# The second block's 116 projection and gate tiles: high weights times both token halves in one 512-column matmul

## What is computed

```
h = rmsnorm(x, norm_w[l])
proj = h @ w_in[l]
a_q, a_f, a_i, a_z, b_x, b_z, c_z, c_xbc, c_dt, gate_logits = jnp.split(proj, split_idx, axis=-1)
...   # three mixers: o_a (HGRN2), o_b (RG-LRU), o_c (SSD)
branch_out = jnp.einsum('bsnc,ncd->bsnd', branches, w_out[l].reshape(N_BRANCH, BRANCH_WIDTH, D_MODEL))
gates = jax.nn.sigmoid(gate_logits.astype(jnp.float32).reshape(bsz, s, N_BRANCH, D_MODEL))
x = x + jnp.sum(gates * branch_out, axis=2).astype(x.dtype)
```

## Time and profile before

| | us |
|---|---|
| median of 3 runs | 4380.95 (4380.47 to 4385.95) |
| the profiled execution | 4382.56 |
| its span in the trace | 4380.8 |
| PE busy in the span | 4246.8 |
| stage with the 232 halves, first to last matmul | 3456.2 to 4218.5 |

### The profile page before, as it was taken

One profiled execution on the slowest core, in us unless ns is written; L12 is line 12 of the kernel. 1 busy time (PEld: TensorE's weight loads), 2 busy tenths in 40 slices (PEclk: granted clock), 3 DMA queues, 4 the chain that ended last, 5 costly groups with the idle time before them and its releaser, 6 DMA issues. The chain is left out here.

```text
span 4380.8 us, 70242 instructions
## 1 busy us (share of the span) xinstructions
PE 4246.8 (97%) x26191; PEld 3613.4 (82%) x26191; DVE 2891.2 (66%) x4957; ACT 1866.3 (43%) x2812; POOL 216.7 (5%) x532
## 2 busy tenths in 40 slices
PE   8999999999998999999999999999999999999999
PEld 1984444968998889888888888788888899999999
DVE  5549875777687665558876665555555567765746
ACT  1520000454763334444455555444444464454534
POOL 0000000000004630000000000000000100200000
PEclk9999999999999999999999999999999899999999
DMA  9457653437876335456655555666666444444454
GB/s 367 159 201 269 239 214 150 141 126 276 287 239 201 102 107 177 157 201 210 208 192 182 183 183 190 217 215 215 215 215 215 151 175 174 145 156 153 172 194 155
DMA packets 211398, 846.34 MB, mean 193 GB/s; under 512 B 67536, under 2 KB 105696, under 8 KB 122096
## 3 DMA queue, kind: packets, MB, share of 16 engines
q1 hardware_dynamic: 211184, 843.37, 55.2%
HBM read 792.85 MB, written 50.45 MB: 192 GB/s over the span
## 5 line engine op out<-in xcount | busy, mean ns | idle before, releaser
L2569 PE MATMUL bank<-rounded,rounded 128*128 128x512 f32 x2048 | 738.2, 403 | 7.6 <-DVE rounded L2715 7.6
L2571 PE MATMUL bank<-rounded,rounded 128*128 128x256 f32 x2048 | 574.3, 280 | 0.0
L3393 PE MATMUL bank<-rounded,rounded 128*128 128x256 f32 x1856 | 533.6, 288 | 9.2 <-DVE rounded L3639 6.0
L3394 PE MATMUL bank<-rounded,rounded 128*128 128x256 f32 x1856 | 526.0, 283 | 0.0
L3395 PE MATMUL bank<-rounded,rounded 128*128 128x256 f32 x1856 | 526.0, 283 | 0.0
L290 DVE TENSOR_TENSOR rounded<-arena,rounded 128x1024 fp32r<-128x1024 f32 x255 | 312.4, 1225 | 306.0 <-ACT rounded L283 306.0
L2569 PEld LDWEIGHTS bank<-rounded,rounded 128*128 128x128 f32 x2048 | 386.9, 189 | 95.3 <-issue 8.1
L3639 DVE TENSOR_TENSOR rounded<-arena,rounded 128x1024 fp32r<-128x1024 f32 x230 | 289.5, 1259 | 241.3 <-ACT rounded L3440 240.6
L205 PE MATMUL bank<-arena 128*128 128x512 f32 x1024 | 443.4, 595 | 2.3 <-PEq L101 2.3
L283 ACT ACTIVATE rounded<-arena 128x1024 fp32r<-128x1024 f32 x255 | 270.6, 1062 | 394.2 <-PE bank L2955 389.2
L2623 ACT ACTIVATE rounded<-arena 128x1024 fp32r<-128x1024 f32 x256 | 271.6, 1061 | 372.0 <-PE bank L2571 370.5
(11 more groups left out here) (499 smaller groups left out, 9164.7 us busy)
## 6 DMA issues: line engine op xcount, KB each, us to landing
arena<-in_w_in SPq DMA_DIRECT2D x244, 1024.0 KB, 4.8
arena<-in_peer_u SPq DMA_DIRECT2D x128, 1024.0 KB, 4.9
arena<-in_peer_v SPq DMA_DIRECT2D x128, 1024.0 KB, 4.8
arena<-in_w_mod SPq DMA_DIRECT2D x96, 1024.0 KB, 6.7
arena<-in_w_out SPq DMA_DIRECT2D x40, 1024.0 KB, 4.8
arena<-in_w_conv_out SPq DMA_DIRECT2D x16, 1024.0 KB, 4.9
arena<-in_w_dn_out SPq DMA_DIRECT2D x16, 1024.0 KB, 4.8
arena<-in_peer_w_q SPq DMA_DIRECT2D x16, 1024.0 KB, 5.3
```

What stands on the lines that cost most here:

```text
L2569: pe.matmul(k.ps[r][:], wh, flat(k.r(pair_slot + 2 * kt, 2)), start=(kt == 0), stop=False, skip_group_check=True)
L2571: mm = pe.matmul(k.ps[r][:, 0:L], wl, k.r(pair_slot + 2 * kt, 1)[:, 0, :], start=False, stop=(kt == KT - 1), skip_group_check=True)
L3393: pe.matmul(out, wh, hi(kt), start=(kt == 0), stop=False)
L3394: pe.matmul(out, wh, lo(kt), start=False, stop=False)
```

## The change

- The activations are kept as alternating slots, high and low of one step side by side (`pair_slot`), so that one matmul can read 512 columns: high and low tokens. The unsplit h moves to slot 112.
- For each step PE runs two matmuls instead of three: the high weights times the 512 columns into the whole bank, and the low weights times the 256 high columns into columns 0 to 255. The columns streamed are the same 768.
- The result is then in two halves of the bank. ACT copies the right half (`carry`), DVE adds the left half to it (`join`), 116 times each; `tile_out` is now counted by DVE.
- The sigmoids of the last 20 gate tiles are no longer part of the copy. ACT does four tiles at a time: four more `gate_act` in this stage (i = 206, 212, 220, 228) and one in the next, for which the last products wait (`last_gates`).

```diff
@@ mixers: PE @@
-                out = k.ps[j % 4][:, 0:L]
+                both, one_ = k.ps[j % 4][:], k.ps[j % 4][:, 0:L]
...
-                    pe.matmul(out, wh, hi(kt), start=(kt == 0), stop=False)
-                    pe.matmul(out, wh, lo(kt), start=False, stop=False)
-                    mm = pe.matmul(out, wl, hi(kt), start=False, stop=(kt == KT - 1))
+                    pe.matmul(both, wh, hi_lo(kt), start=(kt == 0), stop=False, skip_group_check=True)
+                    mm = pe.matmul(one_, wl, hi(kt), start=False, stop=(kt == KT - 1), skip_group_check=True)
@@ mixers: ACT @@
-            def evacuate(j):
+            def carry(j):
                 act.wait_ge(k.half_done, 2 * (s + j + 1))
                 if j == 16:
                     act.wait_ge(x_out, 16)
-                func = ACT.Sigmoid if j >= BEFORE_GATES + PLAIN_GATES else ACT.Copy
-                act.activation(place(j), k.ps[j % 4][:, 0:L], func).then_inc(k.tile_out, 1)
+                act.copy(place(j), k.ps[j % 4][:, L:2 * L]).then_inc(carried, 1)
...
-                act.activation(k.r(hi_slot + 4 * c, 4), k.t(lo_slot + 4 * c, 4), ACT.Copy).then_inc(h_high, 1)
+                act.activation(k.halves(pair_slot + 8 * c, 0, 4), k.t(plain_slot + 4 * c, 4), ACT.Copy).then_inc(h_high, 1)
...
-                if i in (195, 196, 197, 200, 201, 202, 205):
-                    gate_act((195, 196, 197, 200, 201, 202, 205).index(i))
-            evacuate(tiles - 1)
+                if i in (195, 196, 197, 200, 201, 202, 205, 206, 212, 220, 228):
+                    gate_act((195, 196, 197, 200, 201, 202, 205, 206, 212, 220, 228).index(i))
+            carry(tiles - 1)
@@ mixers: DVE @@
+            def join(j):
+                dve.wait_ge(carried, j + 1)
+                dve.tensor_tensor(place(j), k.ps[j % 4][:, 0:L], place(j), ALU.add).then_inc(k.tile_out, 1)
...
             for i in range(halves):
                 if i >= 2:
                     low(i // 2, i % 2)
+                if i % 2 and i > 1:
+                    join(i // 2 - 1)
...
+            join(tiles - 1)
@@ branch_outputs: ACT and DVE @@
+                if i == 12:
+                    x4 = k.t(GATE_AT[2] + 12, 4)
+                    act.activation(x4, x4, ACT.Sigmoid).then_inc(last_gates, 1)
...
+                if b == 2 and m == 12:
+                    dve.wait_ge(last_gates, 1)
```

More of the change, by code:

```diff
@@ L3113, with mixers @@
 PLAIN_GATES = 28
-def mixers(k, w, hi, lo, following3, sum_slot, hi_slot, lo_slot, x_saved):
+def mixers(k, w, following3, sum_slot, pair_slot, plain_slot, x_saved):
     nc = k.nc
@@ L3157, in mixers @@
     total = lambda m: tile(sum_slot, m)
+    hi = lambda kt: k.r(pair_slot + 2 * kt, 1)[:, 0, :]
+    lo = lambda kt: k.r(pair_slot + 2 * kt + 1, 1)[:, 0, :]
+    hi_lo = lambda kt: flat(k.r(pair_slot + 2 * kt, 2))
     root1, inv1, mean2, root2, inv2 = (k.gst[:, m, :] if m < 4 else k.mod_c[:, 0:2] for m in range(5))
@@ L3194, in mixers @@
             "final_done", "x_out"))
+        carried = sem("carried")
         block = stage.enter_context(nc.Block())
@@ L3578, in _ @@
                 if i % 2 and i > 1:
-                    evacuate(i // 2 - 1)
+                    carry(i // 2 - 1)
                 if i in (10, 11, 12, 18, 19, 20):
@@ L3836, in h_scaled @@
             def h_scaled(c):
-                x = k.t(lo_slot + 4 * c, 4)
+                x = k.t(plain_slot + 4 * c, 4)
                 dve.tensor_tensor(x, x, row12.unsqueeze(1).broadcast_to([P, 4, L]), ALU.mult).then_inc(scaled, 1)
@@ L3841, in h_lower @@
                 dve.wait_ge(h_high, c + 1)
-                dve.tensor_tensor(k.r(lo_slot + 4 * c, 4), k.t(lo_slot + 4 * c, 4), k.r(hi_slot + 4 * c, 4),
-                                  ALU.subtract).then_inc(h_low, 1)
+                dve.tensor_tensor(k.halves(pair_slot + 8 * c, 1, 4), k.t(plain_slot + 4 * c, 4),
+                                  k.halves(pair_slot + 8 * c, 0, 4), ALU.subtract).then_inc(h_low, 1)
+            def join(j):
+                dve.wait_ge(carried, j + 1)
+                dve.tensor_tensor(place(j), k.ps[j % 4][:, 0:L], place(j), ALU.add).then_inc(k.tile_out, 1)
             dve.wait_ge(n_act, 2)
@@ L3977, in branch_outputs @@
         sem = lambda n: k.sem(stage, f"final_{n}")
-        x_in, gated, added, squared, prescaled, summed, root, inverted, row_ready, scaled, stored = (sem(n) for n in (
-            "x_in", "gated", "added", "squared", "prescaled", "summed", "root", "inverted", "row_ready",
+        last_gates, x_in, gated, added, squared, prescaled, summed, root, inverted, row_ready, scaled, stored = (sem(n) for n in (
+            "last_gates", "x_in", "gated", "added", "squared", "prescaled", "summed", "root", "inverted", "row_ready",
             "scaled", "stored"))
@@ L4145, in program @@
         w2 = i["w_in_2"]
-        expert_output(k, v, 64, acts_saved, 32, k.mod_x[:, 80:96], x1_saved, w2[0:2], 80, 48)
+        expert_output(k, v, 64, acts_saved, 32, k.mod_x[:, 80:96], x1_saved, w2[0:2], 80, 112)
         wo2 = i["w_out_2"]
-        mixers(k, w2, rounded(32), rounded(48), wo2[0:2], 80, 32, 48, x2_saved)
+        mixers(k, w2, wo2[0:2], 80, 32, 112, x2_saved)
         branch_outputs(k, wo2, 32, x2_saved, k.col("final_w"), out)
```

## The result

The changed kernel takes 4372.18 us (median of 15 executions, 4367.1 to 4375.17) beside 4383.94 us (15 executions, 4377.86 to 4392.17) of the kernel before on the same chip: a ratio of 0.9973, with a 95% interval of 0.9966 to 0.998, or 8.8 to 14.9 us less. On a second chip the two stood at 4367.2 (5 executions) and 4382.6 (24), 0.996 [0.9947, 0.9973]. So it is faster by a little more than 0.2%. The forecast was 4372 us, in a range of 4364 to 4381.

A forecast was written before the change was run, and what follows sets the result against it. The prediction took PE's own time to bound the kernel. It summed -16.4 us (matmuls), +6.6 (DVE's sums) and +0.5 (stage end) to -9.3 us, giving 4372 us from a median of 4380.95, range 4364 to 4381.

The forecast's parts named there:

- The bound: Changed stage: PE leads, busy 756 of 763 us; DVE (498) and ACT (378) follow with room.
- The matmuls, -16.4 us: Each half of the stage 0.071 us shorter over 231 distances, one start and weight load fewer per step; between 12.2 and 23.3.
- the rival built on it: No gain on PE: at most 4.6 us saved, 6.6 + 0.5 lost, 4383.5 us; chance 0.08.
- DVE's sums, +6.6 us: 116 new DVE additions, free in most places, lose 6.6 us where DVE is tight; bounded at 3 and 9.
- the level cycles: Seven cycles, halves 80 to 116, where PE already waits for DVE's `low`: 0.47 us lost each, 3.3 us.
- the reciprocals: Two stretches where DVE has almost no idle time and would lead PE: 1.2 us lost at the first, 0.9 at the second.
- the other tight halves: One more loss at `c_inverse`, 0.3 us, and some nine halves waiting on ACT's or DVE's chain, 0.9 us.
- PE's waits: PE's waits for `low` in the stage grow from 12 to some 30 and from 6 us to some 12.
- The end, +0.5: At the stage's end the last tile's sum comes between the last copy and the next stage's first matmul: 0.5 us lost.
- The slower rate throughout: Whole stage at 2.828 us a half: 12.2 saved, net -5.7, 4375 us, within 0.2%; chance 0.28.
- the faster rate throughout: Whole stage at the faster paired rate: 23.3 saved, 8 lost, net -14.8, 4366 us; chance 0.14.
- DVE as the bound: Each sum's 0.33 us shows in PE's time, 38 us against 16.4: 4402 us; in part or whole, chance 0.08.

The follow-up runs named there:

- joins_twice: Changed kernel with a second DVE instruction of the sum's shape ahead of each of the 116 sums; 4375.87 us, ratio 0.9976 to the kernel before.
- three_matmuls: Changed kernel with its 512-column matmul cut into two of 256, copies, sums and sigmoids kept; 4382.06 us, ratio 1.0 to the kernel before.
- no_joins: Changed kernel without DVE's 116 sums, ACT copying the left half and freeing the bank; 4369.68 us, ratio 0.997 to the kernel before.
- no_gate_sigmoids: Changed kernel without the four late four-tile sigmoids and the next stage's one with its wait; 4371.12 us, ratio 0.9962 to the kernel before.
- grouped_early: Changed kernel, each half's high-weight matmuls first, PE waiting for low weights only between the groups; 4359.24 us, ratio 0.9937 to the kernel before; again 4357.1, 0.9938.

## Why the prediction was right, point by point

- **The bound.** PE leads and the others follow: confirmed by the waits after, and by joins_twice, where even 571 us of DVE leave PE in the lead.
- **The matmuls, -16.4 us.** The mechanism, one matmul less of three for the same columns, is shown by three_matmuls (start and weight load together). The size: the last 80 us run at the slower rate, as this row of the changed kernel shows:

```profile
L3397 PE MATMUL bank<-rounded,rounded x219: 394/399/404, 4127.6 to 4204.7; 128*128 128x512 f32 x110
```

  77.1 / 218 = 0.3537 us a step; the earlier trace rows had 0.3601. Others run at the faster one, as in halves 5 to 7:

```profile
L3397 PE MATMUL bank<-rounded,rounded x24: 392/394/396, 3480.2 to 3488.1; 128*128 128x512 f32 x24
```

  7.9 / 23 = 0.3435 between these rounded ends, or 3 x 2.773 us by the halves, 0.347 a step. The mean gain over the free halves is 11.0 / 166 = 0.066 us (0.076 in the second trace) for the predicted 0.071, both rates mixed as forecast. By 231 distances that is 15.3 us, 17.5 in the second trace.
- **The Trainium skill's formula** (TensorE: Matmul & The Clock Gate, Back-to-back issue gap: 2.5 ns for each matmul in the isolated warm gap) would have given, as an estimate, 4.6 us. The trace does not agree: with the same 768 columns in one matmul less, a step is 6 to 13 ns shorter, and the rival built on it falls with three_matmuls against the changed kernel.
- **DVE's sums, +6.6 us: mechanism right, size off.** Where PE waits for `low` there is no gain, as said, and the places named (halves 50 to 56, 80 to 116, 184 to 188) are the ones. But the loss is smaller. The stage shortened by 11.0 us without the late load; against 15.3 that is 4.3 us lost. If each half at which the 0.066 us did not come counts as a loss of it, the 4.3 us are 1.8 in the level cycles (forecast 3.3), 1.3 at the reciprocals (2.1), 0.6 in the other tight halves (1.2), and 0.7 in the first 18 halves, which had no term. Of the 4.3 about 1.5 are the sums' own (no_joins); the rest is the gain that DVE's old work withholds. The terms that were too large are the level cycles and the reciprocals. In the level cycles I took 0.33 us for the sum in each of the seven, 2.3 us; the changed kernel against no_joins shows 0.2 to 0.4 us for all seven together. DVE's rows there, beside the earlier trace rows, say why:

```profile
3708.12 1.57 DVE L3641 TENSOR_TENSOR rounded<-arena,rounded 128x1024 fp32r<-128x1024 f32 x1 [0.29 <-ACT rounded L3443]
3709.61 0.41 DVE L3849 TENSOR_TENSOR arena<-bank,arena 128x256 f32<-128x256 f32 x1
3709.95 1.45 DVE L3745 TENSOR_TENSOR arena<-arena 128x512 f32<-128x512 f32 x1
3711.32 0.68 DVE L3746 TENSOR_TENSOR arena<-arena 128x512 f32<-128x512 f32 x1
3711.92 1.21 DVE L3641 TENSOR_TENSOR rounded<-arena,rounded 128x1024 fp32r<-128x1024 f32 x1
```

  The first `level` instruction took 1.78 us and takes 1.45, and so it goes on with no sum and with two. POOL's two additions (start, duration of both) and the same `level`, in no_joins:

```profile
3702.37 3.52 POOL L3231 TENSOR_TENSOR arena<-arena 128x512 f32<-128x512 f32 x2 [255.62 <-DVE arena L3759]
3704.67 1.78 DVE L3745 TENSOR_TENSOR arena<-arena 128x512 f32<-128x512 f32 x1
```

  in the changed kernel:

```profile
3707.31 3.53 POOL L3231 TENSOR_TENSOR arena<-arena 128x512 f32<-128x512 f32 x2 [256.49 <-DVE arena L3759]
```

  and in joins_twice:

```profile
3709.72 3.52 POOL L3231 TENSOR_TENSOR arena<-arena 128x512 f32<-128x512 f32 x2 [258.26 <-DVE arena L3759]
3712.68 1.11 DVE L3745 TENSOR_TENSOR arena<-arena 128x512 f32<-128x512 f32 x1
```

  POOL ends at 3705.89, 3710.84 and 3713.24, and `level` at 3706.45, 3711.40 and 3713.79, each time 0.55 or 0.56 us later, whenever it began. So in this place POOL's end sets `level`'s, and the sums fit into time that `level` would have spent beside POOL: they are nearly free here, one or two of them. I had bounded contention from above only. At the reciprocals:

```profile
3613.90 1.16 DVE L3641 TENSOR_TENSOR rounded<-arena,rounded 128x1024 fp32r<-128x1024 f32 x1
3614.98 0.41 DVE L3849 TENSOR_TENSOR arena<-bank,arena 128x256 f32<-128x256 f32 x1
3616.97 1.16 DVE L3641 TENSOR_TENSOR rounded<-arena,rounded 128x1024 fp32r<-128x1024 f32 x1
3619.70 1.16 DVE L3641 TENSOR_TENSOR rounded<-arena,rounded 128x1024 fp32r<-128x1024 f32 x1
```

  5.80 us for two halves, not 5.96. That is 5.47 us and one sum of 0.33, where I had 5.63 for the old work: the second `low` of the earlier trace rows had waited. It took 1.23 us instead of 1.16 and did not overlap the reciprocal before it by 0.08, and I took out only the 0.04 us of idle time. DVE's busy time, 534 us for the forecast 546, is another slip: I added the sums' full durations (48.5), but busy time counts an overlap once, and 116 x 0.33 = 38 would have given 536.
- **PE's waits** were to grow to some 12 us in 30 places; they are 6.4 in 15, and none is shown at halves 50 to 56 or 184 to 188, though these gained nothing. That sign was wrong, and part of the reason is the 0.16 us above: at the reciprocals, where DVE leads by little, a first matmul that is late by less still overlaps its predecessor.
- **The end, +0.5.** From the stage's last matmul to the next stage's first it was 4.35 us from start to start, and is 4.81: +0.46. The rows beside the earlier trace rows:

```profile
4207.67 0.37 ACT L3449 COPY arena<-bank 128x256 f32<-128x256 f32 x1 [4.33 <-PE bank L3398]
4208.08 0.42 DVE L3849 TENSOR_TENSOR arena<-bank,arena 128x256 f32<-128x256 f32 x1 [3.40 <-ACT arena L3449]
4212.16 0.38 PE L4023 MATMUL bank<-rounded,rounded 128*128 128x256 f32 x1 [4.53 <-DVE rounded L4076]
```

- **Not in the sum:** 1.1 us more behind the stage (the clock after pauses, below; the last sigmoid's wait, 0.3), 1.0 us of a later start of the stage in this execution, and the late load of before, -1.4. These nearly cancel. The misses of the sum, 2.3 us too dear on DVE and 1.1 us too large a gain, cancel in part: the stage was to be 9.8 us shorter and is 11.0, and the span is 4380.8 - 4371.0 = 9.8 us shorter, against 9.3 forecast. The start of the sum moved as well. I took the gain of 9.3 us off 4380.95, the median of 3 runs; over 15 runs the kernel before stands at 4383.94, 3.0 us higher, and the measured gain is 11.8, 2.5 us larger. So the closeness of 4372 to 4372.18 is mostly luck, though the gain was within 2.5 us; it differs by more than that from chip to chip (12 and 15 us).
- **The rivals.** The slower rate throughout is right for the last 32 halves and for most stretches before them, but not for all (57 plain halves against 26 at the faster rate); the faster rate throughout is not reached; DVE as the bound is excluded by joins_twice.

## What to carry to other kernels

Price the removal of a small matmul by the distance between starts in the same kernel, and count only the steps at which PE does not wait: here 47 of 231 halves gave nothing, since another engine held them. Take the time from which a gain is subtracted from more than three runs, too, if it is to be good to 3 us. When a change makes the leading engine faster, look first at what it waits for late: a half that uses its high weights first can wait for the low ones in its middle, and that order made the paired form worth 18 us of stage instead of 10 to 12, and the two together 26 (ratio 0.9937, the best kernel of this study). And a short instruction in a busy queue costs its length only if the work behind it is not held by something else anyway, as `level` is by POOL.

## What the runs showed of the hardware

- **The clock after a pause differs from execution to execution.** Behind the 4 us pause at the stage's end the same matmuls start 0.21 us apart instead of 0.12, at half the granted clock, for a while. Stretches right behind the pause (columns as above, the last three granted clock, DMA share, GB/s), before:

```profile
4223.00:4226.00 3.00, 2.91 (x13) 2.91 (x14) 1.17 (x2) 0.00 (x0) 0.00 (x0) 0.50 0.26 44
4226.00:4230.00 4.00, 4.00 (x36) 4.00 (x35) 1.28 (x2) 1.06 (x1) 0.00 (x0) 1.00 1.00 426
```

  and of the changed kernel:

```profile
4212.00:4215.00 3.00, 2.84 (x15) 2.84 (x16) 1.25 (x2) 0.00 (x0) 0.00 (x0) 0.62 0.30 44
4215.00:4217.00 2.00, 2.00 (x15) 2.00 (x15) 0.00 (x0) 0.11 (x1) 0.00 (x0) 0.72 0.90 377
```

  12 distances of 0.21 us before, 16 in the changed kernel (whose first few ran at full clock), 26 in no_gate_sigmoids: some 0.09 us each, 0.4 to 1.3 us of difference between kernels whose pause is alike.
- **One form of matmuls has two steady rates.** Alternating 512 and 256 columns take 0.347 or 0.3535 us a step for whole stretches, without a wait in either. The last 32 halves gain the same 1.7 us in five of the six kernels with that order, while other stretches differ between two traces of one kernel. Grouped, they take 0.349. What chooses between the two in the alternating order is open; no run tried it.
- **A wait's idle time understates its cost:** 0.49 us of idle PE shown, 0.74 us gained when it went, for the reason given at grouped_early.
